# RWKV chunk inverse: products for one of its two forms, 32x32 transposes on VectorE for the other

## Chip, cores and metric

One core of one Trainium2 chip. The metric is the device time of one execution in microseconds (us). Engines are named as the profile names them: PE (TensorE), DVE (VectorE), ACT (ScalarE), POOL (GpSimd), SP (SyncE).

## What is computed

The reference is a stack of two transformer-like blocks over 512 tokens of width 1024, in float32. The change lies in the second block's RWKV mixer, which runs over 256 context tokens and 512 main tokens, forward and backward, with 8 heads of 64:

```python
def step(S, inp):
    r_t, w_t, k_t, v_t, kk_t, b_t = inp
    sa = jnp.einsum('bhvk,bhk->bhv', S, kk_t)
    S = (S * w_t[:, :, None, :] - sa[..., None] * b_t[:, :, None, :]
         + v_t[..., None] * k_t[:, :, None, :])
    return S, jnp.einsum('bhvk,bhk->bhv', S, r_t)
```

Everything else of the two blocks (attention, gating, feed-forward layers) is outside the change.

## The kernel before, in words

The recurrence is done in 12 chunks of 64 tokens (NCH), of which 0 to 3 are context and 4 to 11 main. A chunk of both directions and 8 heads is 16 problems of 64x64. Two heads share a tile's 128 partitions (HEADS), so a tile of eight columns p (four feature groups f for each direction d) holds all 16; `half(d)` is the half of one direction. Inside a chunk, a triangular 64x64 matrix must be inverted. That is done by doubling the size of the inverted blocks: it starts from exact 2x2 blocks, and five levels (LEVELS, lv 0 to 4) take it to 64x64. Level lv needs LOFF[lv], the off-diagonal blocks of that size, which POOL cuts out of the product GB with a mask (function `loff`, L3146 of the profile).

The inverse is held in two forms, Y and its transpose X. At each level and for each direction: PE forms T = LOFF^T X (`t_level`), ACT copies T out of PSUM (L3000), PE forms the corrections of both X and Y from T (`xy_level`), and DVE subtracts them (`update`, L3086, one instruction for X and Y together). The next level's T waits for that. Level 4 corrects Y alone, since X isn't needed after it.

The start values come from two products of their own: `gram_l` gives X, `gram_lt` gives Y, both in level 1 of the chunk before; DVE masks them (`x_init`, L3068 and L3071) and POOL adds the unit matrix (L3156).

PE has two helpers. `by_head` (L2673) issues for each head h a 64x64 product whose input rows and output rows are the same half of the partitions. `crosswise` (L2680) takes its input from one half and writes to the other half. So the two use different 64x64 quarters of PE's array. `turned` (L2819) transposes by a product with the unit and stays in its half.

The order is written out by hand in one loop over n; with m = n - 1 and g = n + 1, the pass of chunk n also does the state and outputs of chunk m and the Gram products of chunk g. On PE, per level: T, with other products (`aside`) put between its instructions; level 0 the products `kv(m)` with the transposes `turn_kb`; level 1 `sa(m)` with `turn_v`; level 2 `outputs(m)` and then `new_state`; levels 3 and 4 `gram` of B and K for chunk g (128 columns wide in main chunks), and `prepare` (rates and running sums, in odd and in even n); then `xy_level`. On DVE: `update` for d = 0 and d = 1, and between them `evacuate` (L3078: Gram products times a mask, out of PSUM), in even n also `rate_products`, `key_products` (L3050) and `products` (L3058 to L3064: three or, for main chunks, four SBUF-only multiplications per direction; d = 0 at the head of level 4, d = 1 after it). POOL: the unit, then the five masks; in even n masks 2 to 4 wait until DVE has done the products of both directions (semaphore `prods`).

In a trace each matmul of this phase counts as two records of PE, since float32 is fed twice.

Of the kernel before, what the change touches and what calls it, by code (L numbers as in the profile page):

```python
# [2676 lines left out]
def crosswise(pe, out, lhsT, rhs, start=True, stop=True):  # L2677

    for h, o in zip(HEADS, HEADS[::-1]):
        mm = pe.matmul(out[o], lhsT[h], rhs[h], start=start, stop=stop)  # L2680
    return mm


def rwkv_loop(k):
# [57 lines left out]
    def tensor(k, pe):  # L2742
# [41 lines left out]
        def gram_l(g):  # L2784
            wait("prods", prep(g // 2, 1))
            if g == 1:
                wait("gk", 1)
            elif g >= 2:
                wait("tok_copied", 3 * (g - 2) + 3)
            for p in range(8):  # L2790
                mm = by_head(pe, k.bank[7][:, column(p)], feature(AR, g, p // 4, p % 4)[:, 0, :], feature(B, g, p // 4, p % 4))
                if p == 7:
                    mm.then_inc(sems["gram_l"], 1)
                yield

        def gram_lt(g):
            if g >= 2:
                wait("tok_copied", 3 * (g - 2) + 2)
            for p in range(8):
                mm = crosswise(pe, k.bank[6][:, column(p)], feature(B, g, p // 4, p % 4), feature(AR, g, p // 4, p % 4)[:, 0, :])  # L2800
            mm.then_inc(sems["gram_lt"], 1)
# [650 lines left out]
```

## Time and profile before

| | us |
|---|---|
| Median of 3 runs (2674.32 to 3305.1) | 2682.56 |
| The profiled execution, its own time | 2680.07 |
| Its span in the profile | 2678.3 |
| Around the span | 1.8 |
| PE busy / DVE / ACT / POOL | 2486.2 / 1350.4 / 512.7 / 144.5 |
| The RWKV loop, from the first `latents` to the last output | about 1794 to 2158, so 364 |

How to read it: busy time is the union of an engine's instructions, and matmuls overlap in PE, so a busy PE need not be full. The chain that ended last is 86% PE over the whole span, most of it in other phases (L1630, L1840, L512). The change touches only the loop between 1794 and 2158, some 14% of the span. "issue" in a row is time in which an engine was idle and nothing that the profile shows held it.

### The profile page before, as it was taken

The page shows a single profiled execution, that of the slowest core. Times are in us where ns is not written, and L with a number is a line of the kernel's source. Part 1 is how long each engine was busy: PE and PEld are TensorE (multiplying, and loading weights), DVE is VectorE, ACT ScalarE, POOL GpSimd, SP SyncE. Part 2 cuts the span into 40 slices and gives each one's busy share as a digit, 9 for nine tenths or more (in the row PEclk, how much of TensorE's full clock was granted, in tenths as well). Part 3 has the DMA queues.
Part 4 walks back from the last instruction along what each step waited for, and adds up shares of the span by engine and source line. Part 5 has one row for each costly group of instructions (what it writes and reads, how often), then busy time and mean ns, then how long its engine had stood idle before and what let it go on. Part 6 is the DMA issues. An engine that isn't in the chain of part 4 may idle for free.

```text
span 2678.3 us, 49291 instructions
## 1 busy us (share of the span) xinstructions
PE 2486.2 (93%) x21560; PEld 1929.4 (72%) x21560; DVE 1350.4 (50%) x2478; ACT 512.7 (19%) x1032; POOL 144.5 (5%) x106
## 2 busy tenths in 40 slices
PE   8989999999999999999998989987887798999997
PEld 5845888888686448888884745457776756888886
DVE  4625555533454336555333264645665435877623
ACT  2121110001003321010001043223333222122100
POOL 0000000000000000000000000003333200000000
PEclk9988999999999999999999989988999998999999
DMA  5323322234120032232233103100000023222132
GB/s 165 129 68 126 95 94 66 73 87 122 48 95 33 1 120 70 95 95 74 77 109 123 48 16 85 32 1 4 4 4 4 4 95 105 84 95 95 45 88 73
DMA packets 221181, 190.53 MB, mean 71 GB/s; under 512 B 8727, under 2 KB 219064, under 8 KB 220968
## 3 DMA queue, kind: packets, MB, share of 16 engines
q1 hardware_dynamic: 220674, 187.29, 22.6%
q8 instruction: 171, 2.80, 0.4%
q14 instruction: 42, 0.34, 0.0%
q10 hardware_dynamic: 294, 0.09, 0.0%
HBM read 185.25 MB, written 2.10 MB: 70 GB/s over the span
## 4 chain that ended last, share of the span: by engine, by line
PE 86%; DVE 6%; issue 3%; ACT 2%; SPq 1%; POOL 1%; DMA 0%; DVEq 0%; POOLq 0%; ACTq 0%
PE psum L1630 30%; PE psum L1840 14%; PE psum L512 8%; PE psum L1130 4%; PE psum L2680 4%; PE psum L2673 3%; PE psum L1344 3%; PE psum L1341 3%; PE psum L3235 2%; PE psum L542 2%; PE psum L1066 1%; DVE sbuf L3086 1%; PE psum L2270 1%; PE psum L2252 1%; PE psum L1109 1%
## 5 line engine op out<-in xcount | busy, mean ns | idle before, releaser
L1630 PE MATMUL psum<-sbuf 128*128 128x256 f32 x3696 | 805.3, 381 | 3.5 <-DVE sbuf L476 1.9
L1630 PEld LDWEIGHTS psum<-sbuf 128*128 128x128 f32 x3696 | 706.8, 191 | 101.7 <-issue 4.3
L1840 PE MATMUL psum<-sbuf 128*128 128x256 f32 x1848 | 403.9, 381 | 11.1 <-DVE sbuf L1858 5.5
L1840 PEld LDWEIGHTS psum<-sbuf 128*128 128x128 f32 x1848 | 352.9, 191 | 61.7 <-DVE sbuf L1858 6.3
L1714 DVE TENSOR_TENSOR sbuf<-sbuf,psum 128x256 f32<-128x256 f32 x462 | 177.9, 418 | 201.0 <-PE psum L1630 199.8
L512 PE MATMUL psum<-sbuf 128*128 128x512 f32 (+3 forms) x688 | 247.9, 519 | 4.3 <-DVEq L617 4.0
L2680 PE MATMUL psum<-sbuf 64*64 64x64 f32 x4992 | 201.7, 228 | 50.8 <-issue 25.9
L2680 PEld LDWEIGHTS psum<-sbuf 64*64 64x64 f32 x4992 | 175.5, 139 | 62.7 <-issue 53.7
L512 PEld LDWEIGHTS psum<-sbuf 128*128 128x128 f32 (+2 forms) x688 | 129.4, 189 | 115.5 <-issue 103.4
L2673 PE MATMUL psum<-sbuf 64*64 64x64 f32 (+1 forms) x4544 | 177.0, 230 | 21.7 <-issue 15.4
L2673 PEld LDWEIGHTS psum<-sbuf 64*64 64x64 f32 x4544 | 160.4, 138 | 28.0 <-issue 18.3
L1876 DVE TENSOR_TENSOR sbuf<-sbuf,psum 128x256 f32<-128x256 f32 x84 | 34.2, 419 | 229.0 <-PE psum L1840 228.6
L427 POOL TENSOR_TENSOR sbuf<-sbuf 128x512 f32<-128x512 f32 x30 | 37.8, 1280 | 1921.1 <-DVE sbuf L413 1920.9
L3086 DVE TENSOR_TENSOR sbuf<-sbuf,psum 128x512 f32<-128x512 f32 (+1 forms) x120 | 73.1, 630 | 114.4 <-PE psum L2673 114.2
L1130 PE MATMUL psum<-sbuf 128*128 128x512 f32 x256 | 117.1, 607 | 0.0
L1650 ACT ACTIVATE sbuf<-sbuf 128x512 f32<-128x512 f32 x44 | 27.7, 630 | 399.7 <-DVE sbuf L1714 399.7
L1130 PEld LDWEIGHTS psum<-sbuf 128*128 128x128 f32 x256 | 48.0, 195 | 53.1 <-issue 53.1
L1700 DVE TENSOR_TENSOR sbuf<-sbuf 128x512 f32<-128x512 f32 x66 | 44.5, 691 | 81.1 <-PE psum L1630 67.1
L1344 PE MATMUL psum<-sbuf 128*128 128x256 f32 x392 | 85.4, 379 | 0.0
L3146 POOL TENSOR_TENSOR sbuf<-sbuf 128x512 f32<-128x512 f32 x60 | 76.7, 1311 | 115.6 <-DVE sbuf L3078 86.1
L1344 PEld LDWEIGHTS psum<-sbuf 128*128 128x128 f32 x392 | 74.2, 190 | 11.3 <-issue 1.3
L1178 DVE TENSOR_REDUCE sbuf<-psum 128x1 f32<-128x256 f32 (+3 forms) x80 | 36.8, 460 | 87.8 <-PE psum L1066 52.0
(280 smaller groups left out, 2698.6 us busy)
## 6 DMA issues: line engine op xcount, KB each, us to landing
sbuf<-in_w_mod_dram SPq DMA_DIRECT2D x24, 1024.0 KB, 5.2
sbuf<-in_w_ffn_gate_dram SPq DMA_DIRECT2D x22, 1024.0 KB, 5.5
sbuf<-in_w_ffn_up_dram SPq DMA_DIRECT2D x22, 1024.0 KB, 7.6
sbuf<-in_w_ffn_down_dram SPq DMA_DIRECT2D x32, 704.0 KB, 6.0
sbuf<-in_w_up_dram SPq DMA_DIRECT2D x22, 1024.0 KB, 7.2
sbuf<-in_w_out_dram SPq DMA_DIRECT2D x12, 1024.0 KB, 7.7
sbuf<-in_w_in_dram SPq DMA_DIRECT2D x12, 1024.0 KB, 5.5
sbuf<-in_w_down_dram SPq DMA_DIRECT2D x16, 704.0 KB, 6.2
```

Of the source, the lines that this page charges most:

```text
L512: mm = pe.matmul(bank, w[:, q, c0:c0 + m], rhs(k0 + q), start=start and q == 0, stop=stop and q == kc - 1)
L542: mm = pe.matmul(bank, act_chunk(q), w[:, q, :], start=q == 0, stop=q == kc - 1)
L1130: mm = pe.matmul(bank_of(b), tiles[b // 2][:, q, (b % 2) * P:(b % 2) * P + P], MIX[:, q, :], start=q == 0, stop=q == KD - 1)
L1341: mm = pe.matmul(self.bank(p)[:, t * P:(t + 1) * P], x[:, q, t * P:(t + 1) * P], w[:, q, :], start=q == 0, stop=q == 3)
L1344: mm = pe.matmul(self.bank(p), w[:, q, :], x[:, q, :], start=q == 0, stop=q == 3)
L1630: mm = pe.matmul(bank, w[:, q, :], rhs[:, q, :], start=q == 0, stop=q == 3)
L1714: dve.tensor_tensor(out, base, bank_of(u, p, t), ALU.add).then_inc(s["added"], 1)
L1840: mm = pe.matmul(bank_of(g, p), wt[:, q, :], rhs_of[p][:, q, :], start=q == 0, stop=q == UNITS - 1)
L2673: mm = pe.matmul(out[h], lhsT[h], rhs[h], start=start, stop=stop)
L2680: mm = pe.matmul(out[o], lhsT[h], rhs[h], start=start, stop=stop)
L3086: dve.tensor_tensor(xy, xy, new, ALU.subtract).then_inc(sems["xy"], 1)
L3146: pool.tensor_tensor(split(LOFF[lv]), split(GB[g % 2][:, :, 0, :]), both_level(lv), ALU.mult).then_inc(sems["loff"], 1)
```

## The change

- `gram_l`, `gram_lt` and `x_init` go. Y's start value is taken by DVE (`y_init`) from the B Gram product that is formed anyway in level 3; X's start value and each level's X come from Y by DVE's `transpose`, which turns each 32x32 block in its place (`turn_y`, two of 128x256 per chunk after the unit is added, and one after each update of levels 0 to 3). Up to level 3 nothing outside the 32x32 diagonal blocks of Y is filled, so this is the whole transpose.
- `xy_level` forms the correction of Y alone; `update` is 256 wide.
- `crosswise` goes. T, `kv` and `sa` use `by_head`.
- DVE takes both halves of GB, and of GK, before the updates of the level; in level 4 the two turns of chunk g stand before them too.
- POOL makes mask 0 at once, then adds the unit to Y (512 instead of 1024 wide), then makes masks 1 to 4 with no wait for `prods`.

```diff
-        def gram_l(g):
-            wait("prods", prep(g // 2, 1))
...
-        def gram_lt(g):
...
         def gram(g, tile, signal):
-            if tile is B:
+            if tile is K:
                 wait("y_init", g + 1)
             else:
-                wait("gb", g + 1)
+                wait("prods", prep(g // 2, 1))
...
-                if lv == 0:
-                    if d == 0:
-                        wait("eye", n + 1)
-                else:
-                    wait("xy", halves(n, lv - 1, d))
+                wait("x_done", halves(n, lv, d))
...
-                    mm = crosswise(pe, k.bank[2 * d][:, column(p % 4)], LOFF[lv][:, p, :], X[n % 2][:, p, :])
+                    mm = by_head(pe, k.bank[2 * d][:, column(p % 4)], LOFF[lv][:, p, :], X[n % 2][:, p, :])
...
-                    if lv < LEVELS - 1:
-                        crosswise(pe, k.bank[2 * d + 1][:, column(p % 4)], Y[n % 2][:, p, :], T[:, p, :])
                     mm = by_head(pe, k.bank[2 * d][:, column(4 + p % 4)], T[:, p, :], Y[n % 2][:, p, :])
...
-                crosswise(pe, o, GK[m % 2][:, p, 0, :], VTK[m % 2][:, p, :], stop=False)
+                by_head(pe, o, GK[m % 2][:, p, 0, :], VTK[m % 2][:, p, :], stop=False)
...
+        def y_init(g):
+            strict = k.psum[:, 512 * 6:512 * 8].rearrange("p (d f w) -> p d f w", d=2, f=4)[:, :, :, 0:CH]
+            dve.tensor_tensor(split(Y[g % 2]), strict, both("y1", CH), ALU.mult).then_inc(sems["y_init"], 1)
+
+        def turn_y(n, d):
+            dve.transpose(flat(X[n % 2][:, half(d), :]), flat(Y[n % 2][:, half(d), :])).then_inc(sems["x_done"], 1)
...
-            dve.tensor_tensor(xy, xy, new, ALU.subtract).then_inc(sems["xy"], 1)
+            y = flat(Y[n % 2][:, half(d), :])
+            dve.tensor_tensor(y, y, k.bank[2 * d][:, 256:512], ALU.subtract).then_inc(sems["xy"], 1)
+            if lv < LEVELS - 1:
+                wait("xy", halves(n, lv, d))
+                turn_y(n, d)
...
+                    evacuate(g, GK, 1, 1).then_inc(sems["gk"], 1)
+                    wait("eye", g + 1)
+                    for d in range(2):
+                        turn_y(g, d)
...
-                xy = XY[g % 2].rearrange("p w a t -> p (w a) t")
-                pool.tensor_tensor(xy, xy, mask(k, "eye", 0, CH).unsqueeze(1).broadcast_to([P, 16, CH]), ALU.add).then_inc(sems["eye"], 1)
-                for lv in range(LEVELS):
-                    if lv == 2 and exps_in(n) is not None:
-                        wait("prods", prep(exps_in(n), 1))
+                pool.tensor_tensor(Y[g % 2], Y[g % 2], mask(k, "eye", 0, CH).unsqueeze(1).broadcast_to([P, 8, CH]), ALU.add).then_inc(
+                    sems["eye"], 1)
+                for lv in range(1, LEVELS):
                     loff(g, lv)
```

On DVE, chunk 6 from level 3 to the head of chunk 7, before (L3078 takes Gram products out, L3086 is the update, L3058 to L3064 the products):

```order
L3078 TENSOR_TENSOR sbuf<-psum,sbuf 128x512 [waits rwkv_gram_b]
L3086 TENSOR_TENSOR sbuf<-sbuf,psum 128x2x256 [waits rwkv_xy_done]
L3078 TENSOR_TENSOR sbuf<-psum,sbuf 128x512
L3086 TENSOR_TENSOR sbuf<-sbuf,psum 128x2x256 [waits rwkv_xy_done]
L3058 TENSOR_TENSOR sbuf<-sbuf 128x8x64 [waits rwkv_exps]
L3060 TENSOR_TENSOR sbuf<-sbuf 128x8x64
L3062 TENSOR_TENSOR sbuf<-sbuf 128x512 [waits rwkv_k_made]
L3064 TENSOR_TENSOR sbuf<-sbuf 128x512 [waits rwkv_kka,dve_steps]
L3078 TENSOR_TENSOR sbuf<-psum,sbuf 128x512 [waits rwkv_gram_k]
L3086 TENSOR_TENSOR sbuf<-sbuf,psum 128x256 [waits rwkv_xy_done]
```

The same place now, from the first update of level 3 on (L3050 the update, L3039 the turn, L3036 `y_init`, L3026 to L3032 the products, L3045 Gram products):

```order
L3050 TENSOR_TENSOR sbuf<-sbuf,psum 128x256 [waits rwkv_xy_done]
L3039 STREAM_TRANSPOSE sbuf<-sbuf 128x256 [waits rwkv_xy]
L3036 TENSOR_TENSOR sbuf<-psum,sbuf 128x512
L3050 TENSOR_TENSOR sbuf<-sbuf,psum 128x256 [waits rwkv_xy_done]
L3039 STREAM_TRANSPOSE sbuf<-sbuf 128x256 [waits rwkv_xy]
L3026 TENSOR_TENSOR sbuf<-sbuf 128x8x64 [waits rwkv_exps]
L3028 TENSOR_TENSOR sbuf<-sbuf 128x8x64
L3030 TENSOR_TENSOR sbuf<-sbuf 128x512 [waits rwkv_k_made]
L3032 TENSOR_TENSOR sbuf<-sbuf 128x512 [waits rwkv_kka,dve_steps]
L3045 TENSOR_TENSOR sbuf<-psum,sbuf 128x512 [waits rwkv_gram_k]
L3045 TENSOR_TENSOR sbuf<-psum,sbuf 128x512
L3039 STREAM_TRANSPOSE sbuf<-sbuf 128x256 [waits rwkv_eye]
```

Two turns and `y_init` now stand among the updates of level 3, and one more Gram copy and two turns between the products and the first update of level 4.

On PE, a main chunk, the end of level 3's Gram product, the running sums (L2758) and `xy_level`, before:

```order
L2680 MATMUL psum<-sbuf 64x64 x2
L2673 MATMUL psum<-sbuf 64x128 x2
L2758 MATMUL psum<-sbuf 128x128 x8
L2680 MATMUL psum<-sbuf 64x64 x2
L2673 MATMUL psum<-sbuf 64x64 x2
L2680 MATMUL psum<-sbuf 64x64 x2
L2673 MATMUL psum<-sbuf 64x64 x2
```

and now (the running sums are L2751):

```order
L2673 MATMUL psum<-sbuf 64x64 x2
L2673 MATMUL psum<-sbuf 64x128 x2
L2751 MATMUL psum<-sbuf 128x128 x8
L2673 MATMUL psum<-sbuf 64x64 x18
L2673 MATMUL psum<-sbuf 64x128 x2
```

The pairs of L2680 and L2673 that alternated eight times in `xy_level` are now 16 of L2673 (the last two of the 18 are the next level's T), and T in level 3 and 4 stands on L2673 too, between the Gram products.

On POOL, four chunks, now (L3123 adds the unit, L3114 makes masks; before it was L3156 128x1024 and then L3146 x5 in each chunk):

```order
L3114 TENSOR_TENSOR sbuf<-sbuf 128x512 x5
L3123 TENSOR_TENSOR sbuf<-sbuf 128x512
L3114 TENSOR_TENSOR sbuf<-sbuf 128x512 x5
L3123 TENSOR_TENSOR sbuf<-sbuf 128x512
L3114 TENSOR_TENSOR sbuf<-sbuf 128x512 x5
```

Of each five, four belong to the chunk whose unit stands ahead of them, and the last is mask 0 of the next one.

## Rows read from the trace of the kernel before

**Rows 1.** Groups by line and form, 1794:2158; count, busy us, mean ns, idle before it.
```profile
L2680 PE MATMUL psum<-sbuf 64*64 64x64 f32 x4992 | 201.7, 228 | 50.8 <-issue 25.9 <-DVE sbuf L3086 23.0 <-ACT sbuf L3004 0.7
...
L2673 PE MATMUL psum<-sbuf 64*64 64x64 f32 x4032 | 147.4, 225 | 20.3 <-issue 15.4 <-DVE sbuf L3064 3.3 <-DVE sbuf L3071 0.8
```

**Rows 2.** Busy time by stretch: length, then PE, PEld, DVE, ACT, POOL, clock, DMA.
```profile
1794.00:2158.00 364.00, 282.81 (x10917) 260.58 (x10918) 198.76 (x314) 123.32 (x264) 106.53 (x72) 0.95 0.02 4
1983.18:1984.95 1.77, 1.77 (x128) 1.77 (x128) 1.77 (x4) 0.83 (x3) 0.00 (x0) 1.00 0.04 9
1983.18:1986.80 3.62, 1.98 (x128) 1.84 (x128) 1.98 (x4) 1.85 (x4) 0.00 (x0) 1.00 0.02 5
...
2036.27:2037.17 0.90, 0.90 (x32) 0.90 (x32) 0.26 (x1) 0.86 (x2) 0.90 (x2) 1.00 0.00 0
2033.19:2034.96 1.77, 1.77 (x60) 1.72 (x60) 0.54 (x1) 0.38 (x1) 1.74 (x2) 1.00 0.00 0
```

**Rows 3.** Timeline of PE: start us, us; at the end idle before and releaser.
```profile
1977.53 0.68 PE L2680 MATMUL psum<-sbuf 64*64 64x64 f32 x16
...
2007.22 0.68 PE L2680 MATMUL psum<-sbuf 64*64 64x64 f32 x16 [1.79 <-DVE sbuf L3086]
...
2036.18 1.15 PE L2673 MATMUL psum<-sbuf 64*64 64x64 f32 x32
2037.47 0.68 PE L2680 MATMUL psum<-sbuf 64*64 64x64 f32 x16
```

**Rows 4.** Timeline of ACT, copy of one half of T.
```profile
2007.94 0.38 ACT L3000 ACTIVATE sbuf<-psum 128x256 f32<-128x256 f32 x1 [1.89 <-PE psum L2680]
```

**Rows 5.** Timeline of DVE: start of the loop, updates of chunks 1 and 6.
```profile
1802.85 0.69 DVE L3064 TENSOR_TENSOR sbuf<-sbuf 128x512 f32<-128x512 f32 x1
...
1806.96 0.69 DVE L3071 TENSOR_TENSOR sbuf<-psum,sbuf 128x512 f32<-128x512 f32 x1 [0.65 <-PE psum L2680]
...
1844.42 1.29 DVE L3086 TENSOR_TENSOR sbuf<-sbuf,psum 128x512 f32<-128x512 f32 x2 [2.37 <-PE psum L2673]
...
1860.35 0.69 DVE L3086 TENSOR_TENSOR sbuf<-sbuf,psum 128x512 f32<-128x512 f32 x1 [1.57 <-PE psum L2673]
...
1999.96 0.69 DVE L3086 TENSOR_TENSOR sbuf<-sbuf,psum 128x512 f32<-128x512 f32 x1 [1.04 <-PE psum L2673]
```

**Rows 6.** Timeline of DVE, products and what follows them, chunks 6 and 7.
```profile
1989.72 3.44 DVE L3050 SCALAR_TENSOR_TENSOR sbuf<-sbuf 128x512 f32<-128x512 f32 x2
...
2001.76 1.39 DVE L3058 TENSOR_TENSOR sbuf<-sbuf 128x512 f32<-128x512 f32 x1
2003.07 1.75 DVE L3060 TENSOR_TENSOR sbuf<-sbuf 128x512 f32<-128x512 f32 x1
2004.74 0.68 DVE L3062 TENSOR_TENSOR sbuf<-sbuf 128x512 f32<-128x512 f32 x1
2005.46 0.69 DVE L3064 TENSOR_TENSOR sbuf<-sbuf 128x512 f32<-128x512 f32 x1
2006.07 0.68 DVE L3078 TENSOR_TENSOR sbuf<-psum,sbuf 128x512 f32<-128x512 f32 x1
2006.67 0.41 DVE L3086 TENSOR_TENSOR sbuf<-sbuf,psum 128x256 f32<-128x256 f32 x1
...
2031.85 0.69 DVE L3086 TENSOR_TENSOR sbuf<-sbuf,psum 128x512 f32<-128x512 f32 x1 [1.05 <-PE psum L2673]
```

**Rows 7.** Timeline of POOL, the unit added (L3156) and the level masks (L3146).
```profile
1989.94 2.67 POOL L3156 TENSOR_TENSOR sbuf<-sbuf 128x1024 f32<-128x1024 f32 x1 [10.49 <-DVE sbuf L3071]
2001.33 2.95 POOL L3146 TENSOR_TENSOR sbuf<-sbuf 128x512 f32<-128x512 f32 x2 [8.71 <-DVE sbuf L3078]
...
2033.22 6.19 POOL L3146 TENSOR_TENSOR sbuf<-sbuf 128x512 f32<-128x512 f32 x5 [9.19 <-DVE sbuf L3078]
```

**Rows 8.** Busy time by stretch around a wait of chunk 2, clock in it.
```profile
1892.00:1900.00 8.00, 6.68 (x282) 6.58 (x286) 5.17 (x11) 2.49 (x6) 3.74 (x3) 0.79 0.01 2
```

More of the change, by code:

```diff
@@ L2674, in by_head @@
     return mm
[L2677 to L2681, printed above, removed]
 def rwkv_loop(k):
@@ L2704, in rwkv_loop @@
     sems = {n: k.sem(f"rwkv_{n}") for n in (
-        "latent_done", "rated", "cums_done", "exps", "k_gain", "kka", "k_made", "prods", "gram_l", "gram_lt", "gram_b", "gram_k", "x_init", "y_init",
+        "latent_done", "rated", "cums_done", "exps", "k_gain", "kka", "k_made", "prods", "gram_b", "gram_k", "y_init", "x_done",
         "gb", "gk", "loff", "eye", "t_done", "t_copied", "xy_done", "xy", "turned", "tok_copied", "kv_done", "kv_copied",
@@ L2782, in feature @@
             return tile[buf][d][:, f, c]
-        def gram_l(g):
-            wait("prods", prep(g // 2, 1))
[L2786 to L2794, printed above, removed]
-        def gram_lt(g):
[L2797 to L2801, printed above, removed]
         def gram(g, tile, signal):
-            if tile is B:
+            if tile is K:
                 wait("y_init", g + 1)
             else:
-                wait("gb", g + 1)
+                wait("prods", prep(g // 2, 1))
+                if g == 1:
+                    wait("gk", 1)
+                elif g >= 2:
+                    wait("tok_copied", 3 * (g - 2) + 3)
             for p in range(8):
@@ L2885, in sa @@
             for p in range(8):
[L2886 removed]
+                mm = by_head(pe, k.bank[4][:, column(p)], Y[m % 2][:, p, :], KV[:, p, :])
                 next(aside, None)
@@ L2927, in tensor @@
                 aside = nothing
-                if lv == 1 and g < NCH:
-                    aside = gram_l(g)
-                elif lv == 2 and m >= 0:
+                if lv == 2 and m >= 0:
                     aside = outputs(m)
@@ L3064, in products @@
             dve.tensor_tensor(Bf, rate, Bf, ALU.mult).then_inc(sems["prods"], 1)
-        def x_init(g):
-            wait("gram_l", g + 1)
-            dve.tensor_tensor(split(X[g % 2]), k.bank[7].rearrange("p (d f t) -> p d f t", d=2, f=4), both("x1", CH),
-                              ALU.mult).then_inc(sems["x_init"], 1)
-            wait("gram_lt", g + 1)
-            dve.tensor_tensor(split(Y[g % 2]), k.bank[6].rearrange("p (d f t) -> p d f t", d=2, f=4), both("y1", CH),
-                              ALU.mult).then_inc(sems["y_init"], 1)
+        def y_init(g):
[3 more added lines that the diff above has]
+            dve.transpose(flat(X[n % 2][:, half(d), :]), flat(Y[n % 2][:, half(d), :])).then_inc(sems["x_done"], 1)
         def evacuate(g, tile, d, slot):
@@ L3105, in vector @@
             for lv in range(LEVELS):
-                if lv == 4 and exps_in(n) is not None:
-                    products(exps_in(n), 0)
                 if lv == 3 and g < NCH:
@@ L3110, in vector @@
                     evacuate(g, GB, 0, 0)
+                    evacuate(g, GB, 1, 0).then_inc(sems["gb"], 1)
+                if lv == 4 and exps_in(n) is not None:
+                    products(exps_in(n), 0)
                 if lv == 4 and g < NCH:
@@ L3123, in vector @@
                     rate_products(exps_in(n))
-                if lv == 1 and g < NCH:
-                    x_init(g)
                 if lv == 1 and exps_in(n) is not None:
```

15 lines of the change are left out of this document (3 added, 12 removed).

## The prediction

> **What bounds the kernel now.** I read first the groups of the page by line, which put all that the change touches between 1794 and 2158 us, then the groups of that stretch [rows 1], then short stretches of it one by one [rows 2], and last the timelines of PE, ACT, DVE and POOL through one even and one odd chunk [rows 3 to 7].
>
> The loop takes 364 us, in which PE is busy 283 us with some 10,900 records [rows 2]. That is 30 us per chunk: the T of level 0 starts at 1977.53, 2007.22 and 2037.47 in chunks 6, 7 and 8 [rows 3], so chunk 6 took 29.69 and chunk 7 took 30.25 us.
>
> Three things limit it. (a) PE's array. Where `crosswise` and `by_head` alternate, 128 records go in 1.77 us, 13.8 ns each; where only `by_head` stands, 32 take 0.90 us, 28.1 ns each [rows 2]. (b) Something ahead of the array. The quick 128 are followed by 1.85 us with nothing at all, so 128 records take 3.62 us, again 28.3 ns each [rows 2]; the idle time put down to "issue" is 25.9 + 15.4 us in the two groups [rows 1]. PE gets its instructions at about 28 ns per record, whatever the array could do. (c) The chain PE, ACT, DVE, PE inside a level, and DVE alone at the end of even chunks: there PE sits idle 1.79 us for the update [rows 3].
>
> DVE and POOL get in each other's way when both only read SBUF. POOL's two masks at 2001.33 took 2.95 instead of 2 x 1.24 (five take 6.19) [rows 7], and the products beside them 1.39 and 1.75 instead of 0.68; the two L3050 took 3.44 beside the unit [rows 6, 7]. They take turns: one product, one mask. The copies out of PSUM show no such wait: 0.68 [rows 6].
>
> **Removed and added on PE.** Per chunk go 64 X corrections and 32 of `gram_l` and `gram_lt`, 96 matmuls or 192 records, 2304 in 12 chunks. What stays is a stream of one kind at 28.1 to 28.4 ns. So for streams that were mixed, the pace stays: the array slows down to what the supply gave already. I take that pace for all that remains. Where wide Gram products covered T, T's 32 records are now added to them: 0.9 us, since 60 records of both kinds took 1.77 [rows 2].
>
> The Trainium skill ("TensorEngine Tiling (Array Packing)", Tiling Modes, Key Properties) says that tiles of the array load and multiply independently, in parallel. Rows 2 agree, and by that rule alone the removed products were free and the change takes parallel work away; that result is the first rival.
>
> **A turn on DVE.** No row shows a transpose. An update of 256 columns takes 0.41 us and the next instruction starts 0.33 later; a dependent one starts 0.72 instead of 0.60 after a 512-wide one [rows 6], so 0.12 more. The nearest row for 128x256 is that update: I take 0.42 us for the turn. Above, I allow 0.9, twice that; below, 0.3. Update to T was 0.69 + 0.14 = 0.83 (0.14 from 2007.08 to 2007.22 [rows 3, 6]). Now it is 0.45 + 0.42 + 0.14 = 1.01 for d = 0 and, with four instructions in a row, 1.79 for d = 1. The skill ("VectorE: DVE Perf Modes", The three transpose paths) gives 311 ns for 128x128 in bf16; by it a turn would lie near my value, and the sum would not move.
>
> **From T of level 0 to the first update of level 3, main chunk.** 32 records are 0.91; the last records take 0.22 longer and ACT or DVE 0.05 to start [rows 3, 4].
> - Level 0: T 0.91, `kv` and turns 128 records 3.64, 16 of xy 0.46, 0.27: 5.28.
> - Level 1: 1.79, half of T 0.46, `sa` and turns 1.82, 0.73: 4.80.
> - Level 2: 1.01, T and outputs 128 records 3.64, 0.73: 5.38.
> - Level 3: rest of xy 0.19, state 1.82, T and wide Gram 0.91 + 1.77, sums or rates 0.95, 0.73: 6.37.
>
> That is 21.83. Before, it was 1999.96 - 1977.53 = 22.43 in chunk 6 and 2031.85 - 2007.22 = 24.63 in chunk 7 [rows 3, 5, 6], on average 23.5. Gain 1.7 for each of 7 main chunks, 12 us. In context chunks there are no outputs and level 2 becomes the bare chain: 1.01 + T 0.68 + ACT 0.04 + 0.38 + 0.14 + xy 0.73 = 2.98 [rows 3, 4], with the later second half 3.2; level 3 is 5.5. Levels 1 to 3 are then 13.5 against 15.93 in chunk 1 [rows 5]. I keep 1.8 of these 2.4, as level 0 grows somewhat against its best time before. Chunk 4 is alike (its outputs aside belong to a context chunk): 5 x 1.8 = 9 us. Together -21.
>
> **From the first update of level 3 to the next T, odd chunk.** Before 2037.47 - 2031.85 = 5.62 [rows 3, 6]. Now the K Gram product waits for `y_init`, 0.45 + 0.33 + 0.60 + 0.12 = 1.5 after the update. T and Gram end at 4.1. DVE takes GK from 4.4 to 5.6, turns to 6.3, updates, and T starts at 6.9. So +1.3. It holds in the five odd chunks 1 to 9 and in chunk 10: +8.
>
> **The same in even chunks.** Before 7.26 [rows 3, 5]. Update, turn, `y_init`, update, turn take 2.16 until the products may start (before 1.80). POOL, released 1.8 us earlier as both GB halves are taken first, is then at the unit until 2.85, and behind it stand masks 1 to 4 with no wait, 5 us of work. So not two but all four products find POOL in the way. The first costs 1.2, each next one 1.67 (3060 to 3062 [rows 6]): products end at 8.4 after the update, 6.2 us long against 4.31 (2001.76 to 2006.07). Behind them two copies 1.2, two turns 0.66, update and start 0.55: T at 10.8. That is +3.5, of which 1.9 is POOL. Chunks 2, 4, 6, 8: +14; chunk 0 with three products: +2. Together +16. The earlier cost beside the unit (L3050) goes, but there PE still had the new state to form, so nothing.
>
> **The clock.** PE ends at 5.9 in these and waits until 10.8, 4.9 us. Around the 2.2 us wait of chunk 2 the granted clock averages 0.79 over 8 us [rows 8], so for 3.4 of them it was at 1.2 GHz instead of 2.4. At that level a stream of one kind loses half of 3.4 us; a mixed one didn't. Five waits: 0 to 8.5, I take 6, as they are all longer than the one that did it.
>
> **Start.** The last product ends at 1803.54 and `x_init` at 1807.65 [rows 5]; only then the B Gram product came, now it comes at once. Of 4.1 us the unit and turns take back one: -3.
>
> Sum: -21 + 8 + 16 + 6 - 3 = +6. The profiled execution took 2680.07, 2.5 below the median; forecast **2686**. About 2% (54 us) is what a measurement of this kernel can tell from no change; 54 us is 15% of the loop.
>
> **Bounds.** A turn at 0.3: 6 on the path of a chunk, -0.12 each, -9. At 0.9: +0.45, twice in levels 0 to 3 (the second half counts in part) and two in level 4: 4.5 per chunk, +54. Clock 0 to 8.5. POOL's part 0 to 9.5. The pace: if the supply adds its 41 us of "issue" idle to the slower streams in part, +15.
>
> **Rivals.**
> - *The array decides (slower).* If the 1.85 us behind 128 records isn't a matter of their number but comes whatever the array does, mixed streams lose their overlap: `kv` 1.82, `sa`, outputs' T, and two Gram products' T 0.91 each, 5.5 per chunk, less 0.9 for `gram_lt`: 12 x 4.6 = +55; with the even ends +16 it is 2680 + 71 = 2751. It decides as soon as a block of 128 takes over 4.5 us. Against it: stretches with 1.98 us of busy PE took 3.62 [rows 2]. Chance 0.07.
> - *The turn is dear (slower).* As under bounds, at 0.9: 2740. It passes 54 us only from there. Nothing in the rows speaks for it or against it. Chance 0.07, half of it over 2%.
> - *Only the count matters (faster).* 2304 records x 28.1 ns = 65 us, if PE were never waiting for the chain: 2615. For it: PE idle before matmuls is only 71 us, most of it issue [rows 1]. Against it: with 20% less PE work per chunk the chain comes to light. Chance 0.06.
> - *POOL doesn't do what the change says:* its masks end before the products start or come after them, no turn taking, waits of 3 us: -9 and -6, 2671. For it: exps may be late. Against it: 6 POOL instructions need 7.4 us from GB on. Chance 0.15.
> - The forecast: 0.65.
>
> Range 2655 to 2728. Faster by over 2%: 0.06. Within: 0.84. Slower: 0.10.
>
> **What would show it.** In the trace after: records per stretch 28 ns, with little "issue"; L3039 about 0.42; four products in even chunks with 1.2 to 1.7 us each and POOL's masks between them; PE idle about 5 us before T in even chunks, under 1 in odd ones; T to update 3 about 22 us. Wrong if PE has idle "issue" time beside 28 ns, if turns last over 0.6, or if even and odd chunks take the same time (forecast 32.6 and 28.7).

## The result and the profile after

| | before | after |
|---|---|---|
| Median, us | 2682.56 | 2696.97 (2693.9 to 2701.73, 5 runs) |
| Ratio to before | | 1.0071, 95% interval 1.0057 to 1.0085 |
| Profiled execution / span | 2680.07 / 2678.3 | 2695.64 / 2693.8 |
| Loop, from DVE's first memset to its last | 369.3 | 380.7 |
| Instructions / matmul records of PE | 49291 / 21560 | 44786 / 19256 |

The forecast was 2686 (2655 to 2728), most likely within 2%. The changed kernel is 0.7% slower, inside that. The ratio is taken from the fast executions alone (one of five of the kernel before took 3305.1 us); the quotient of the two medians would be 1.0054. Of the 15.5 us by which the span grew, 11.4 are the loop; 2.5 lie ahead of it and 1.6 behind it, in code that is the same.

Groups by line and form over the loop of the changed kernel: count, busy us, mean ns, idle before it (they answer to [rows 1]; L3039 is the turn, L3050 the update, L3114 the masks).

```profile
L2673 PE MATMUL psum<-sbuf 64*64 64x64 f32 x6720 | 279.9, 224 | 54.5 <-DVE sbuf L3050 24.8 <-DVE sbuf L3039 20.3 <-POOL sbuf L3114 3.8
...
L3114 POOL TENSOR_TENSOR sbuf<-sbuf 128x512 f32<-128x512 f32 x60 | 83.2, 1412 | 616.5 <-DVE sbuf L3045 616.5
...
L3039 DVE STREAM_TRANSPOSE sbuf<-sbuf 128x256 f32<-128x256 f32 x120 | 51.9, 440 | 3.3
L3050 DVE TENSOR_TENSOR sbuf<-sbuf,psum 128x256 f32<-128x256 f32 x120 | 47.6, 403 | 115.0 <-PE psum L2673 114.6
```

On PE "issue" is gone from the first releasers: DVE's update and turn (24.8 + 20.3 us) have taken its place. A turn takes 0.44 us.

Busy time by stretch, the columns of [rows 2]: the loop; chunk 6 from T of level 0 to the first update; the same start in chunk 7; and the end of chunk 6.

```profile
1794.00:2172.00 378.00, 318.94 (x8623) 302.06 (x8624) 212.26 (x424) 123.74 (x264) 97.84 (x72) 0.94 0.01 3
1982.26:1987.65 5.39, 5.39 (x185) 5.39 (x187) 0.19 (x2) 1.35 (x4) 0.96 (x1) 1.00 0.02 6
2015.40:2022.40 7.00, 7.00 (x187) 7.00 (x189) 2.74 (x6) 1.42 (x4) 0.00 (x0) 0.76 0.02 5
2008.00:2015.40 7.40, 3.16 (x73) 2.76 (x69) 7.37 (x10) 2.03 (x5) 6.20 (x4) 1.00 0.00 1
```

The 185 records of the second row take 5.39 us, 29.1 ns each, one behind the other. In the third the granted clock averages 0.76: TensorE ran at 1.2 GHz for part of it. In the fourth, just ahead of it, PE has 73 records in 7.4 us.

Timeline of DVE in chunk 6, the answer to [rows 5] and [rows 6]: first updates of levels 0, 1, 2, 3, then the end of the chunk (L3036 `y_init`, L3026 to L3032 the products, L3045 GK).

```profile
1987.64 0.42 DVE L3050 TENSOR_TENSOR sbuf<-sbuf,psum 128x256 f32<-128x256 f32 x1 [5.20 <-PE psum L2673]
1988.10 0.45 DVE L3039 STREAM_TRANSPOSE sbuf<-sbuf 128x256 f32<-128x256 f32 x1
...
1992.45 0.42 DVE L3050 TENSOR_TENSOR sbuf<-sbuf,psum 128x256 f32<-128x256 f32 x1 [0.74 <-PE psum L2673]
...
1997.95 0.42 DVE L3050 TENSOR_TENSOR sbuf<-sbuf,psum 128x256 f32<-128x256 f32 x1 [2.64 <-PE psum L2673]
...
2004.68 0.42 DVE L3050 TENSOR_TENSOR sbuf<-sbuf,psum 128x256 f32<-128x256 f32 x1 [0.42 <-PE psum L2673]
2005.13 0.45 DVE L3039 STREAM_TRANSPOSE sbuf<-sbuf 128x256 f32<-128x256 f32 x1
2005.50 0.65 DVE L3036 TENSOR_TENSOR sbuf<-psum,sbuf 128x512 f32<-128x512 f32 x1
2006.08 0.40 DVE L3050 TENSOR_TENSOR sbuf<-sbuf,psum 128x256 f32<-128x256 f32 x1
2006.52 0.45 DVE L3039 STREAM_TRANSPOSE sbuf<-sbuf 128x256 f32<-128x256 f32 x1
2006.88 1.16 DVE L3026 TENSOR_TENSOR sbuf<-sbuf 128x512 f32<-128x512 f32 x1
2007.97 1.75 DVE L3028 TENSOR_TENSOR sbuf<-sbuf 128x512 f32<-128x512 f32 x1
2009.64 1.76 DVE L3030 TENSOR_TENSOR sbuf<-sbuf 128x512 f32<-128x512 f32 x1
2011.43 1.63 DVE L3032 TENSOR_TENSOR sbuf<-sbuf 128x512 f32<-128x512 f32 x1
2012.99 1.28 DVE L3045 TENSOR_TENSOR sbuf<-psum,sbuf 128x512 f32<-128x512 f32 x2
2014.19 0.76 DVE L3039 STREAM_TRANSPOSE sbuf<-sbuf 128x256 f32<-128x256 f32 x2
2014.88 0.71 DVE L3050 TENSOR_TENSOR sbuf<-sbuf,psum 128x256 f32<-128x256 f32 x2
```

Timeline of POOL at the same place (L3123 adds the unit), the answer to [rows 7].

```profile
2004.33 1.26 POOL L3114 TENSOR_TENSOR sbuf<-sbuf 128x512 f32<-128x512 f32 x1 [21.12 <-DVE sbuf L3045]
2006.23 1.27 POOL L3123 TENSOR_TENSOR sbuf<-sbuf 128x512 f32<-128x512 f32 x1 [0.64 <-DVE sbuf L3036]
2007.46 6.74 POOL L3114 TENSOR_TENSOR sbuf<-sbuf 128x512 f32<-128x512 f32 x4
```

Timeline of PE, T of level 0 in chunks 7 and 8, the answer to [rows 3].

```profile
2015.40 1.49 PE L2673 MATMUL psum<-sbuf 64*64 64x64 f32 x36 [4.24 <-DVE sbuf L3050]
...
2046.15 1.05 PE L2673 MATMUL psum<-sbuf 64*64 64x64 f32 x29 [0.30 <-DVE sbuf L3050]
```

The four products take 6.2 us (2006.88 to 2013.06) with POOL's four masks between them (6.74 us for 4), and PE waits 4.24 us for DVE. In odd chunks that wait is 0.30 us.

Start of T of level 0 to the first update of level 3, and from there to the next T, worked out from the starts of these rows in each chunk, in us:

| chunk | before | after | forecast |
|---|---|---|---|
| 1 (context) | 20.74 + 4.89 | 19.26 + 5.82 | |
| 4 | 21.49 + 7.27 | 20.08 + 10.72 | |
| 5 | 23.42 + 5.63 | 23.87 + 6.78 | 21.83 + 6.9 |
| 6 | 22.43 + 7.26 | 22.42 + 10.72 | 21.83 + 10.8 |
| 7 | 24.63 + 5.62 | 23.97 + 6.78 | 21.83 + 6.9 |
| 8 | 24.37 + 7.26 | 22.42 + 10.73 | 21.83 + 10.8 |

### The profile page after: what moved, and what is told of

The parts are those of the page before. It is cut to its first block, busy times and chain, and to the rows that moved or that the text cites. A ratio compares the mean times of both kernels' runs of the same rounds, so it can differ in the third digit from the quotient of the medians.

```text
span 2693.8 us, 44786 instructions
## 1 busy us (share of the span) xinstructions
PE 2524.6 (94%) x19256; PEld 1971.4 (73%) x19256; DVE 1363.4 (51%) x2586; ACT 512.4 (19%) x1032; POOL 135.8 (5%) x106
## 4 chain that ended last, share of the span: by engine, by line
PE 87%; DVE 7%; issue 2%; ACT 1%; SPq 1%; POOL 1%; DMA 1%; DVEq 0%; POOLq 0%; ACTq 0%
PE psum L1630 30%; PE psum L1840 14%; PE psum L512 8%; PE psum L2673 8%; PE psum L1130 4%; PE psum L1344 3%; PE psum L1341 3%; PE psum L3201 2%; PE psum L542 2%; PE psum L2797 1%; PE psum L1066 1%; PE psum L2270 1%; DVE sbuf L3039 1%; PE psum L2252 1%; DVE sbuf L3050 1%
## 5 line engine op out<-in xcount | busy, mean ns | idle before, releaser
L1630 PEld LDWEIGHTS psum<-sbuf 128*128 128x128 f32 x3696 | 706.2, 191 | 101.4 <-issue 4.3
L1840 PEld LDWEIGHTS psum<-sbuf 128*128 128x128 f32 x1848 | 353.8, 192 | 62.1 <-DVE sbuf L1858 6.3
L2673 PE MATMUL psum<-sbuf 64*64 64x64 f32 (+1 forms) x7232 | 289.3, 227 | 55.7 <-DVE sbuf L3050 24.8
L2673 PEld LDWEIGHTS psum<-sbuf 64*64 64x64 f32 x7232 | 269.2, 139 | 69.0 <-issue 36.1
L1714 DVE TENSOR_TENSOR sbuf<-sbuf,psum 128x256 f32<-128x256 f32 x462 | 177.9, 417 | 200.0 <-PE psum L1630 198.7
L1876 DVE TENSOR_TENSOR sbuf<-sbuf,psum 128x256 f32<-128x256 f32 x84 | 34.2, 419 | 231.1 <-PE psum L1840 230.6
L427 POOL TENSOR_TENSOR sbuf<-sbuf 128x512 f32<-128x512 f32 x30 | 37.8, 1277 | 1923.2 <-DVE sbuf L413 1923.0
L3114 POOL TENSOR_TENSOR sbuf<-sbuf 128x512 f32<-128x512 f32 x60 | 83.2, 1412 | 616.5 <-DVE sbuf L3045 616.5
L3050 DVE TENSOR_TENSOR sbuf<-sbuf,psum 128x256 f32<-128x256 f32 x120 | 47.6, 403 | 115.0 <-PE psum L2673 114.6
L1130 PEld LDWEIGHTS psum<-sbuf 128*128 128x128 f32 x256 | 48.0, 195 | 53.1 <-issue 53.1
L1344 PEld LDWEIGHTS psum<-sbuf 128*128 128x128 f32 x392 | 74.2, 190 | 11.3 <-issue 1.3
L2968 ACT ACTIVATE sbuf<-psum 128x256 f32<-128x256 f32 x120 | 46.0, 383 | 167.9 <-PE psum L2673 167.1
L1341 PEld LDWEIGHTS psum<-sbuf 128*128 128x128 f32 x672 | 75.4, 192 | 0.1
```

The lines of the kernel that those rows point to most:

```text
L1130: mm = pe.matmul(bank_of(b), tiles[b // 2][:, q, (b % 2) * P:(b % 2) * P + P], MIX[:, q, :], start=q == 0, stop=q == KD - 1)
L1341: mm = pe.matmul(self.bank(p)[:, t * P:(t + 1) * P], x[:, q, t * P:(t + 1) * P], w[:, q, :], start=q == 0, stop=q == 3)
L1344: mm = pe.matmul(self.bank(p), w[:, q, :], x[:, q, :], start=q == 0, stop=q == 3)
L1630: mm = pe.matmul(bank, w[:, q, :], rhs[:, q, :], start=q == 0, stop=q == 3)
L1714: dve.tensor_tensor(out, base, bank_of(u, p, t), ALU.add).then_inc(s["added"], 1)
L1840: mm = pe.matmul(bank_of(g, p), wt[:, q, :], rhs_of[p][:, q, :], start=q == 0, stop=q == UNITS - 1)
```

## The experiments

"One diagonal" below means that all products of a stream use the two quarters of PE's array whose input half and output half are the same; a mixed stream uses all four.

Each is compared with the kernel before on the same chip: its medians were 2680.17 beside e1 to e4, 2677.57 beside e5, e6, e7 and e10, and 2677.27 beside e9 and e11. Half the width of a ratio's interval is 3 to 6 us. The changed kernel's 2696.97 stood beside a median of 2682.56, so a difference "to the changed kernel" below holds 2 to 5 us that can lie between the occasions; by the ratios the differences are 14 us for e1, 23 for e4, 56 for e5, 21 for e7 and for e10, and 35 for e11. The loop in each trace, from DVE's first memset to its last, doesn't have that uncertainty: 369.3 before and 380.7 after, then 370.8 (e1), 397.2 (e2), 333.6 (e3), 359.9 (e4), 438.3 (e5), 361.2 (e6), 361.2 (e7), 356.7 (e9), 403.8 (e10) and 346.7 (e11).

### e1: POOL waits for the products again

```diff
                 for lv in range(1, LEVELS):
+                    if lv == 2 and exps_in(n) is not None:
+                        wait("prods", prep(exps_in(n), 1))
                     loff(g, lv)
```

> The changed kernel, but POOL waits again, in even chunks, for DVE's products of both directions before masks 2 to 4. My theory (POOL's masks without a wait make all four products of an even chunk take turns, and the long wait of PE that follows costs clock): two of the four products (one of three in chunk 0) are released, 1.05 us each, so the stretch from the first update of level 3 to the next T in chunks 2, 4, 6, 8 goes from 10.7 to 8.6 us, in chunk 0 from 8.5 to 7.5: -9 us, and up to -4 more if the clock drops fewer times; the changed kernel's 2697 becomes 2684 to 2688. Rival (the even ends are bound by something else, or POOL's masks then come too late for level 2 and later of the next chunk): within 3 us of 2697.

Measured 2685.77 (2682.09 to 2693.34), ratio 1.0020 (1.0008 to 1.0032). Timeline of DVE in chunk 6, the four products:

```profile
2003.60 1.16 DVE L3026 TENSOR_TENSOR sbuf<-sbuf 128x512 f32<-128x512 f32 x1
2004.69 1.75 DVE L3028 TENSOR_TENSOR sbuf<-sbuf 128x512 f32<-128x512 f32 x1
2006.36 0.68 DVE L3030 TENSOR_TENSOR sbuf<-sbuf 128x512 f32<-128x512 f32 x1
2007.08 0.69 DVE L3032 TENSOR_TENSOR sbuf<-sbuf 128x512 f32<-128x512 f32 x1
```

and of POOL, mask 1 and then mask 2 of the next chunk:

```profile
2004.18 1.71 POOL L3114 TENSOR_TENSOR sbuf<-sbuf 128x512 f32<-128x512 f32 x1
2012.89 1.26 POOL L3114 TENSOR_TENSOR sbuf<-sbuf 128x512 f32<-128x512 f32 x1 [7.00 <-DVE sbuf L3032]
```

Two products still take turns with the unit and mask 1, the other two are down to 0.68 and 0.69. T comes 8.70 us after the update instead of 10.72. So the early masks cost 2.0 us in each even chunk. The clock gives back little: the starts of chunks 3 and 9 are down to 6.93 us from 7.72 and 7.75, but those of chunks 5 and 7 stay at 6.93 (6.83 and 6.94 in the changed kernel), though PE now waits 2.22 us ahead of them instead of 4.24. In all 11 us, of which 9 are the even ends.

### e4: the products behind level 4

```diff
-                if lv == 4 and exps_in(n) is not None:
-                    products(exps_in(n), 0)
...
             if exps_in(n) is not None:
+                products(exps_in(n), 0)
                 products(exps_in(n), 1)
```

> The changed kernel with the products of both directions of an even chunk behind the last update of level 4, instead of d = 0 at the head of level 4. My theory: the even ends become like the odd ones (10.7 to 6.8 us in chunks 2, 4, 6, 8, 8.5 to 6 in chunk 0), POOL's masks are nearly done before the products begin, PE no longer waits over 4 us and the clock doesn't fall in the odd chunks' level 0 (6.8 to 7.7 back to 5.4): -18 and -8, so 2697 becomes 2668 to 2676, under the kernel before. Rival (the products are then late for level 0's update, or the clock falls for another reason): 2685 or more.

Measured 2675.23 (2670.37 to 2681.02), ratio 0.9984 (0.9973 to 0.9996), 22 us below the changed kernel. Timeline of DVE, the end of chunk 6:

```profile
2001.12 0.45 DVE L3039 STREAM_TRANSPOSE sbuf<-sbuf 128x256 f32<-128x256 f32 x1
2003.64 1.29 DVE L3045 TENSOR_TENSOR sbuf<-psum,sbuf 128x512 f32<-128x512 f32 x2 [2.07 <-PE psum L2673]
2004.84 0.76 DVE L3039 STREAM_TRANSPOSE sbuf<-sbuf 128x256 f32<-128x256 f32 x2
2005.53 0.71 DVE L3050 TENSOR_TENSOR sbuf<-sbuf,psum 128x256 f32<-128x256 f32 x2
2006.16 1.41 DVE L3026 TENSOR_TENSOR sbuf<-sbuf 128x512 f32<-128x512 f32 x1
2007.50 0.68 DVE L3028 TENSOR_TENSOR sbuf<-sbuf 128x512 f32<-128x512 f32 x1
```

Behind the turn at 2001.12 GK is copied as soon as PE has it, and the products begin after the last update. T comes 6.78 us after the update in even chunks as in odd ones. Busy time from T of level 0 in chunk 7, which came after that shorter wait:

```profile
2006.06:2011.96 5.90, 5.81 (x192) 5.67 (x192) 5.83 (x10) 2.19 (x7) 0.97 (x1) 1.00 0.02 6
```

5.90 us at a full clock, against 6.94 in the changed kernel: without the long wait the clock didn't fall in this odd chunk. The 0.51 us above the 5.39 of an even chunk are the price of the move. DVE is busy for 5.83 of the 5.90 us in that row, and the first update (2011.95) stands right behind the last of the eight products; the rival had named this. Behind the first rise at the loop's start the clock fell once in the loop, against four times in the changed kernel. That one fall came in level 1 of chunk 3 (6.35 us instead of 4.80, granted clock 0.73), behind waits of 0.15 and 1.93 us, so a long wait isn't the only thing that stands ahead of a fall.

### e6: the same move in the kernel before

The diff is e4's, on the kernel before.

> The kernel before with the products of d = 0 moved behind level 4's last update. If the gain of this move belongs to the changed kernel alone, because POOL's early masks and four slow products stood there: under 3 us. By the walk of the rows, the even ends go from 7.26 to 5.62 as in odd chunks, five times 1.6 us: 5 to 9 us less than 2680, that is 2671 to 2675. If later products hold up the B Gram product or the next chunk's level 1, the same or slower.

Measured 2670.7 (2663.41 to 2676.19), ratio 0.9970 (0.9957 to 0.9983): 6.9 us. The even ends fell from 7.26 to 5.62. So this much of e4's 22 us lay in the old kernel too; the other 15 came with the change, which put POOL's masks and two turns there. Of the kernels here that leave nothing out it has the lowest median; e9's interval (0.9971 to 0.9990) overlaps with its own (0.9957 to 0.9983).

### e5: every turn twice

```diff
         def turn_y(n, d):
+            k.dve.link(dve.transpose(flat(X[n % 2][:, half(d), :]), flat(Y[n % 2][:, half(d), :])))
             dve.transpose(flat(X[n % 2][:, half(d), :]), flat(Y[n % 2][:, half(d), :])).then_inc(sems["x_done"], 1)
```

> The changed kernel with every turn done twice in a row, the second linked behind the first, 120 more in all (what is computed stays the same). Theory, that the turns stand on the chain from update to T: the extra one costs its 0.44 us and the link, some 0.49 us; d = 0's in full in levels 0 to 3, d = 1's where DVE itself is late, and both of the next chunk's at the head of level 4: 3.5 to 5 us per chunk, so 42 to 59 us more than the changed kernel's 2697, that is 2738 to 2756. Rival, that PE's stream of records hides most of a turn: under 20 us more, below 2717.

Measured 2754.37 (2751.07 to 2755.65), ratio 1.0278 (1.0262 to 1.0294): 57 us above the changed kernel. Groups of DVE, the turns added and the old ones:

```profile
L3040 DVE STREAM_TRANSPOSE sbuf<-sbuf 128x256 f32<-128x256 f32 x120 | 53.5, 445 | 4.1
L3039 DVE STREAM_TRANSPOSE sbuf<-sbuf 128x256 f32<-128x256 f32 x120 | 52.8, 440 | 3.3
```

120 more turns of 0.44 us are 53 us of DVE, and 57 us came on the time, as the theory had it, but not all of it by the turns' own length. At a full clock a main chunk grew by 0.96 us in level 1, 0.48 in level 2, nothing in levels 0 and 3 and 1.43 to 1.50 at its end: 2.9 us for ten turns of 0.445, where the theory had put 3.5 to 5. The rest stands where the clock is low:

```profile
2016.83:2024.14 7.31, 5.72 (x135) 5.47 (x132) 4.89 (x11) 2.40 (x7) 0.00 (x0) 0.77 0.02 4
```

This is level 1 of chunk 6, 7.31 us at 0.77 where others take 5.76 at a full clock. The steps at a low clock, added up over the loop, come to some 27 us, against 8 in the changed kernel. So of the 57 us about 38 are turns on the chain and about 19 the clock behind the waits that they lengthen; that the sum met the theory is in part luck. The first turn of a level isn't worth as much, since it came with a shorter update.

### e3: the kernel before without X's corrections

```diff
-                    if lv < LEVELS - 1:
-                        crosswise(pe, k.bank[2 * d + 1][:, column(p % 4)], Y[n % 2][:, p, :], T[:, p, :])
```

The update is 256 wide; X keeps its start value, so this leaves out X's corrections.

> The kernel before without the products that correct X and with updates 256 wide; it leaves the corrections of X out (X stays at its start value). What the removal alone is worth. My theory (each record costs 28 ns of supply wherever it stands, even in a free quarter): 128 records per chunk, 3.6 us, of which the chains of levels 1 to 3 and the DVE-bound even ends keep a part: -22 to -38 us on 2682. Rival (the removed products ran in quarters that were free, and cost nothing): only the shorter update shows, 0.27 us per level: -8 to -13 us.

Measured 2645.12 (2643.86 to 2647.61), ratio 0.9869 (0.9852 to 0.9886): 35 us for 1536 records and the narrower update, 23 ns per record if all of it is put down to them; what the update alone is worth wasn't run. That is far above the 8 to 13 us of the rival: the products that were removed had a price.

### e10: the Gram products of level 1 put back

```diff
+        def gram_again(g):
...
+            for p in range(8):
+                by_head(pe, k.bank[7][:, column(p)], feature(AR, g, p // 4, p % 4)[:, 0, :], feature(B, g, p // 4, p % 4))
+                yield
+            for p in range(8):
+                by_head(pe, k.bank[6][:, column(p)], feature(B, g, p // 4, p % 4), feature(AR, g, p // 4, p % 4)[:, 0, :])
...
+                if lv == 1 and g < NCH:
+                    aside = gram_again(g)
-                if lv == 2 and m >= 0:
+                elif lv == 2 and m >= 0:
```

> The changed kernel with the products of gram_l and gram_lt put back where they stood, in level 1, both on one diagonal, 64 records per chunk (nobody reads them; what is computed stays the same). Theory, that level 1 is a plain stream at 28.4 ns per record: 4.80 becomes 6.6 us, 1.8 per chunk, 20 to 23 us more than 2697, that is 2717 to 2720. Rival, that they fit into PE's waits inside level 1 (for the copies of T and of KV): less than 8 us more.

Measured 2719.57 (2718.5 to 2721.82), ratio 1.0149 (1.0132 to 1.0166): 23 us above the changed kernel. From the first update of level 0 to that of level 1 it took 6.44 instead of 4.80, 1.64 for 64 records. Over the chunks that is 18 of the 23 us; the rest are starts of chunks at a lower clock (8.00 instead of 6.83 in chunk 5). With e3, what the change removed is worth some 58 us when taken alone, close to the 65 of the rival that only the count matters. So the question is what took it all back.

### e2: one diagonal in the kernel before

```diff
-    for h, o in zip(HEADS, HEADS[::-1]):
+    for h, o in zip(HEADS, HEADS):
         mm = pe.matmul(out[o], lhsT[h], rhs[h], start=start, stop=stop)
```

Count, order and waits stay, what `crosswise` forms lands in its own half, so X, Y, KV and SA hold the wrong heads.

> The kernel before with crosswise writing to the same half as by_head, so the count and order of instructions stay and only the second pair of array quarters goes unused. My theory (PE gets instructions at about 28 ns per record, so most of the overlap of quarters was worth nothing): +15 to +35 us on 2682, mostly T beside the wide Gram products (0.9 us in levels 3 and 4) and the short bursts behind a wait. Rival (the array decides alone): every mixed stream doubles: kv 1.8, sa 0.9, outputs 0.9, gram_l 0.9, two Grams 1.8, X and Y corrections 3.6 per chunk, about 10 us per chunk, +100 us or more.

Measured 2712.96 (2710.22 to 2717.02), ratio 1.0122 (1.0099 to 1.0145): 33 us, at the upper end of what I had given. Busy time in chunk 6 from T of level 0 to the first update:

```profile
1994.59:2000.82 6.23, 6.07 (x200) 5.94 (x202) 0.78 (x2) 1.81 (x5) 1.10 (x1) 1.00 0.01 3
```

6.23 us, in every main chunk, where the kernel before took 3.93 to 5.36. The loop grew by less than the whole, 27.8 us. Here my picture began to give way: if the supply of instructions set the pace of mixed streams, this would have cost little.

### e7: mixed streams in levels 0 and 1 of the changed kernel

```diff
-            for h, i in zip(HEADS, ident):
-                mm = pe.matmul(k.bank[bank][h, column(p)], rows[h], i, start=True, stop=True)
+            for h, o, i in zip(HEADS, HEADS[::-1], ident):
+                mm = pe.matmul(k.bank[bank][o, column(p)], rows[h], i, start=True, stop=True)
...
-                        tokens_copied(3 * m + 2, KTK, 6)
-                        tokens_copied(3 * m + 3, BTK, 7, -1.0)
+                        tokens_copied(3 * m + 2, KTK, 6, 0.0)
+                        tokens_copied(3 * m + 3, BTK, 7, 0.0)
```

> The changed kernel with the transposes by a product with the unit (turned) written to the other half of the partitions, so that in levels 0 and 1 streams of both kinds mix again as before; KTK and BTK are scaled by 0 (the state stays zero and the heads of V are exchanged, so this leaves the state's part of the output out; the count and the shapes of instructions are the same). Theory, that the supply of instructions at 28 ns per record sets these levels and the array only where the clock has dropped: T of level 0 to the first update stays 5.4 in even chunks and falls from 6.8 to 7.8 to about 5.4 in chunks 3, 5, 7 and 9: 5 to 12 us less than 2697. Rival, that the array's one diagonal sets them: 1.5 us or more less per chunk and level, 30 to 45 us less. If neither the array nor the clock matters there: within 3 us.

Measured 2675.89 (2671.14 to 2681.85), ratio 0.9991 (0.9981 to 1.0001): 21 us below the changed kernel, between my 5 to 12 and the rival's 30 to 45. Busy time of the same start in chunks 6 and 7:

```profile
1978.74:1982.26 3.52, 3.50 (x177) 3.36 (x177) 0.19 (x2) 1.24 (x3) 0.97 (x1) 1.00 0.02 5
2009.73:2014.72 4.99, 4.99 (x184) 4.99 (x186) 2.68 (x6) 1.24 (x3) 0.00 (x0) 0.67 0.01 3
```

In chunk 6, 3.52 us for 177 records, 19.9 ns each and T among them, where the changed kernel needs 5.39. My theory had said 5.4. The supply can give far more than one record in 28 ns here; the one diagonal made the pace. In chunk 7, where the granted clock is 0.67, the same mixed streams take 4.99: they lose to the clock as well.

### e11: T, kv and sa crosswise again

```diff
-                    mm = by_head(pe, k.bank[2 * d][:, column(p % 4)], LOFF[lv][:, p, :], X[n % 2][:, p, :])
+                    mm = crosswise(pe, k.bank[2 * d][:, column(p % 4)], LOFF[lv][:, p, :], X[n % 2][:, p, :])
...
-                by_head(pe, o, GK[m % 2][:, p, 0, :], VTK[m % 2][:, p, :], stop=False)
+                crosswise(pe, o, GK[m % 2][:, p, 0, :], VTK[m % 2][:, p, :], stop=False)
```

and so for the second product of `kv` and for `sa`; the helper `crosswise` is put back.

> The changed kernel with T, kv and sa written crosswise as in the kernel before, while turned, the Gram products, outputs, the state and Y's corrections stay in their half (nothing is exchanged back, so Y and all that follows come out for the wrong head; count, shapes and waits are those of the changed kernel). e7 mixed levels 0 and 1 alone and took 21 us off. Theory, that the array's one diagonal costs wherever two kinds stood side by side: T's 0.9 us beside the outputs of level 2 (8 chunks) and beside the B Gram product of level 3 (11 chunks) go too, up to 17 us: 2659, between 2655 and 2668. Rival, that the supply at 28 ns per record takes over after what e7 had: 2676 within 4.

Measured 2660.99 (2658.86 to 2664.37), ratio 0.9942 (0.9929 to 0.9955): 36 us below the changed kernel, as the theory had it (2659), and 15 below what the supply as a limit would have left. Busy time by stretch, the loop and the start of chunk 6:

```profile
1794.00:2140.00 346.00, 270.23 (x8628) 250.38 (x8626) 212.83 (x424) 125.36 (x266) 97.91 (x72) 0.92 0.01 3
1969.73:1973.20 3.47, 3.47 (x177) 3.33 (x177) 0.18 (x1) 1.20 (x3) 1.78 (x2) 1.00 0.02 5
```

and its groups of PE over the loop:

```profile
L2680 PE MATMUL psum<-sbuf 64*64 64x64 f32 x3072 | 136.6, 237 | 53.0 <-DVE sbuf L3057 28.0 <-DVE sbuf L3046 19.8 <-POOL sbuf L3121 3.8
L2673 PE MATMUL psum<-sbuf 64*64 64x64 f32 x3648 | 130.2, 225 | 13.3 <-issue 8.6 <-DVE sbuf L3039 3.3 <-ACT sbuf L2986 0.7
```

The number of records is that of the changed kernel, 8628 against 8623, and the loop, 380.7 us in the changed kernel, takes 346.7. "Issue" is back, but with 8.6 us against 41 before. So the halves alone turn a change that would have gained 0.6% into one that loses 0.7%. In this form the kernel forms another result, since the pieces meet in different halves; whether one can be built that turns on DVE and still mixes wasn't tried.

### e9: y_init first

On e4's kernel:

```diff
                     evacuate(g, GB, 1, 0).then_inc(sems["gb"], 1)
+                    y_init(g)
...
-                if lv == 3 and g < NCH:
-                    y_init(g)
```

> The kernel of e4 (products of d = 0 last) with y_init directly behind the two copies of GB, ahead of the updates of level 3. Theory, that the K Gram product waits for y_init in every chunk: DVE is idle before that update for some time, so the first update of level 3 comes at most 0.6 us later and the K Gram product starts earlier; the end from the first update of level 3 to the next T falls from 6.78 to 5.7 to 6.2, net 0.3 to 0.8 us less per chunk: 3 to 9 us less than e4's 2675, that is 2666 to 2672. Rival, that the update is on the chain in full and the Gram product isn't: 0 to 6 us more than 2675.

Measured 2671.64 (2668.2 to 2681.05), ratio 0.9980 (0.9971 to 0.9990). In chunks 3 to 8 the first update of level 3 came 0.09 us later and T 6.39 instead of 6.78 after it: 0.3 per chunk, at the lower end of what I had given. In chunks 9 and 10 it went the other way: the update came 0.6 us later and T 8.01 after it instead of 6.77, at a granted clock of 0.79 in chunk 9's end. The intervals of e4 and e9 overlap, so the whole run doesn't show the 3.6 us between the medians (1 us by the ratios).

## Why the prediction came out right, and where it didn't

- **From T to the first update of level 3.** The steps were forecast as 5.28, 4.80, 5.38 and 6.37; chunk 6 has 5.39, 4.81, 5.50 and 6.73. Context chunks: level 2 2.94 against 2.98, level 3 6.13 to 6.95 against 5.5. Level 3 was short by 0.36 in chunks 5 to 8 and by 0.6 to 1.45 in chunks 1 to 4, together 5 us. It is the mis-sized term, and with it the gain of 21 us came out at some 17, clock left out: the 5.5 was put down without a walk of its own, and chunks 3 and 4 have wide Gram products already.
- **Odd ends**: 6.78 for 6.9. **Even ends**: 10.72 for 10.8, with the four products and the masks one after the other as the rows had said. e1 measures POOL's part at 2.0 for the 1.9. The rival that POOL would not overlap (2671) falls.
- **The clock.** Starts of chunks 3, 5, 7 and 9 took 7.72, 6.83, 6.94 and 7.75 instead of 5.39: 7.7 us for the 6 forecast. e4 ties it to the wait ahead: without the wait the start of chunk 7 took 5.90, at a full clock. That a mixed stream loses nothing was wrong (e7, 3.52 to 4.99), and the kernel before had shown it already (below).
- **The start**: the T of chunk 1 stands 46.1 us behind the first memset against 51.1; -5.0, where -3 for the start, +2 and -1.8 in chunk 0 make -2.8.
- **Even against odd chunks**: 33.14 and 30.7, forecast 32.6 and 28.7; the odd ones carry the clock, which the sum had, but this pair of numbers hadn't.
- **The turn**: 0.44 us for 0.42. The dear turn falls. Another 0.44 us per turn cost 57 us in e5, the clock's part with it, so at 0.9 a turn would have cost about the 54 that the rival said.
- **The loop** came to +11.4 for +6, and the profiled execution to 2695.64 for 2686.

The step that was wrong in its reason, though not in its numbers, is this: "So for streams that were mixed, the pace stays: the array slows down to what the supply gave already." One diagonal at 28 ns was right, and the steps came out of it. That the supply gave no more than one record in 28 ns was not, and the trace of the kernel before could have told. Its starts of chunks 6 and 5, from T of level 0 to the first update:

```profile
1977.53:1981.46 3.93, 3.77 (x214) 3.64 (x217) 0.78 (x2) 1.27 (x4) 1.92 (x2) 1.00 0.01 4
1948.48:1953.73 5.25, 5.25 (x214) 5.07 (x216) 3.28 (x6) 1.26 (x4) 1.85 (x2) 0.67 0.01 3
```

In chunk 6, 214 records go in 3.93 us, 18.4 ns each and with hardly a gap; in chunk 5 the same mixed stream, at a granted clock of 0.67, takes 5.25. The forecast gave this stage 5.28 in the changed kernel, 1.35 longer than chunk 6 took before, with fewer records in it (185 in the trace after). What holds a mixed stream back goes with how many records are asked for over a longer stretch. The kernel before asks for one in 33 ns on average (10917 in 364 us), and its two large groups of products are idle for 41 us on "issue"; without X's corrections (e3) it is one in 35 ns (9379 in 328 us), and 16.5 us:

```profile
L2680 PE MATMUL psum<-sbuf 64*64 64x64 f32 x3456 | 145.5, 229 | 26.4 <-DVE sbuf L3084 15.8 <-issue 6.4 <-ACT sbuf L3002 0.7
L2673 PE MATMUL psum<-sbuf 64*64 64x64 f32 x4032 | 143.1, 224 | 17.7 <-issue 10.1 <-DVE sbuf L3062 3.3 <-ACT sbuf L2986 2.4
```

In e11 it is one in 40 ns, and 8.6 us. The changed kernel asks for one in 44 ns (8623 in 378 us), so mixed streams would have run faster in it, as e7 and e11 show. I had held the old average of 23.5 us against the new walk, so the loss went into the small gain of 1.7 per chunk and was not seen as one. What lies behind the "issue" time, some limit of the supply with a store of instructions ahead of PE, no row shows; that stays argued. The rival that the array decides had the direction, and e2 and e11 give it 33 and 36 us; it had put 55, and its whole (2751) came out too high because it took nothing off for the removed work. The Trainium skill ("TensorEngine Tiling (Array Packing)", Key Properties) says that tiles of the array work independently; e7 agrees (3.52 against 5.39 us). What I had drawn from it, that the removed products were free, e3 doesn't bear out: 35 us.

Where the expected gain went, each taken alone and in us: removed products -35 (e3, with the narrower update) and -23 (e10, with its part of the clock); lost mixing +36 (e11); the products' place and POOL's early masks, with their clock, +22 (e4), of which 7 was there before (e6); the rest is the turns, of which e5 gives only the price of a second one. These don't add up to the result exactly, since each was measured with the others in place.
